# S5 state operators multiplied in turned layout from a table of power factors, instead of turned tile by tile

## What is computed

```python
lam_bar = jnp.exp(lam * dt)
b_bar = ((lam_bar - 1.0) / lam)[..., None] * b
...
bu = jnp.einsum("gnp,btgp->btgn", b_bar, u_chunk.astype(jnp.complex64))
_, xs = lax.associative_scan(binop, (a, bu), axis=1)
xs = xs + pow_t[None] * state[:, None]
y = jnp.real(jnp.einsum("gpn,btgn->btgp", c, xs))
```

## Time and profile before

| | us |
|---|---|
| median of 3 runs (2041.51 to 2043.51) | 2042.86 |
| the profiled execution's own time | 2042.9 |
| its span in the trace | 2041.2 |
| PE busy | 2001.8 (98% of the span) |
| DVE busy | 1583.4 (78%) |
| ACT busy | 1127.8 (55%) |
| POOL busy | 575.6 (28%) |
| tile 0 of down projection 0 starts on PE at | 899.1 |
| its last product ends at | about 1153.7 |

### The profile page before, as it was taken

How to read it: one execution, slowest core, us unless ns; L and a number is a source line. 1 busy time by engine, 2 the same in 40 slices (tenths; PEclk the granted TensorE clock), 3 DMA queues, 4 the chain that set the end, 5 groups by cost and what they waited for, 6 DMA issues and landing times.

```text
span 2041.2 us, 40986 instructions
## 1 busy us (share of the span) xinstructions
PE 2001.8 (98%) x13240; PEld 1747.0 (86%) x13240; DVE 1583.4 (78%) x2216; ACT 1127.8 (55%) x1655; POOL 575.6 (28%) x725
## 2 busy tenths in 40 slices
PE   7999999999999999999999889999999999999998
PEld 7877888888888888888888788888888888888886
DVE  7976678987888888878888887788888888865554
ACT  6544455466666656655555435665665655644443
POOL 8999014930000000037666682100000000001110
PEclk9999999999999999999999999999999999999999
DMA  6554535566666555557777995555555555566664
GB/s 239 164 186 166 165 125 172 189 194 206 213 213 200 188 191 186 188 167 238 234 235 236 309 244 189 189 200 189 186 189 190 186 191 189 182 185 192 186 192 133
DMA packets 147453, 398.82 MB, mean 195 GB/s; under 512 B 23344, under 2 KB 48688, under 8 KB 147392
## 3 DMA queue, kind: packets, MB, share of 16 engines
q1 hardware_dynamic: 126752, 379.30, 57.9%
q10 hardware_dynamic: 20640, 18.75, 2.8%
HBM read 377.02 MB, written 18.87 MB: 194 GB/s over the span
## 4 chain that ended last, share of the span: by engine, by line
PE 86%; POOL 8%; DVE 3%; issue 1%; ACT 1%; DMA 1%; ACTq 0%; SPq 0%; DVEq 0%; POOLq 0%
PE bank L389 50%; PE bank L388 25%; PE bank L385 3%; PE bank L386 1%; DVE lo L365 1%; PE bank L2092 1%; PE bank L2094 1%; PE bank L2093 1%; POOL nt L733 1%; DMA uu<-yg 1%; POOL ut L958 1%; POOL nt L734 1%; POOL nt L732 1%; POOL nt L735 1%; ACT hi L358 0%
## 5 line engine op out<-in xcount | busy, mean ns | idle before, releaser
L365 DVE TENSOR_TENSOR lo<-raw,hi 128x1024 fp32r<-128x1024 f32 x698 | 890.0, 1281 | 184.1 <-ACT hi L358 171.0
L358 ACT ACTIVATE hi<-raw 128x1024 fp32r<-128x1024 f32 x698 | 733.9, 1057 | 389.8 <-PE bank L389 332.9
L389 PE MATMUL bank<-aa,hi 128*128 128x512 f32 x2544 | 890.1, 392 | 0.0
L389 PE MATMUL bank<-xx,hi 128*128 128x512 f32 x2236 | 783.9, 392 | 0.0
L388 PE MATMUL bank<-aa,lo 128*128 128x256 f32 x2544 | 711.7, 280 | 0.0
L388 PE MATMUL bank<-xx,lo 128*128 128x256 f32 x2236 | 626.5, 280 | 0.9 <-DVE lo L365 0.9
L389 PEld LDWEIGHTS bank<-aa,hi 128*128 128x128 f32 x2544 | 477.4, 188 | 100.5
L389 PEld LDWEIGHTS bank<-xx,hi 128*128 128x128 f32 x2236 | 419.6, 188 | 87.3
L388 PEld LDWEIGHTS bank<-aa,lo 128*128 128x128 f32 x2544 | 478.7, 188 | 6.2 <-DVE lo L365 0.3
L388 PEld LDWEIGHTS bank<-xx,lo 128*128 128x128 f32 x2236 | 421.1, 188 | 8.4 <-DVE lo L365 2.2
L403 ACT ACTIVATE lowt<-bank 128x256 f32<-128x256 f32 x212 | 81.1, 383 | 208.6 <-PE bank L389 202.0
(11 more groups left out here) (384 smaller groups left out, 1902.6 us busy)
## 6 DMA issues: line engine op xcount, KB each, us to landing
raw<-in_up SPq DMA_DIRECT2D x344, 512.0 KB, 3.2
raw<-in_down SPq DMA_DIRECT2D x160, 448.0 KB, 3.5
raw<-in_w_in SPq DMA_DIRECT2D x98, 512.0 KB, 4.2
raw<-in_w_out SPq DMA_DIRECT2D x32, 512.0 KB, 3.3
raw<-in_down SPq DMA_DIRECT2D x32, 512.0 KB, 4.3
raw<-in_glu SPq DMA_DIRECT2D x32, 512.0 KB, 3.8
s_c<-cp ACTq DMA_DIRECT2D x16, 256.0 KB, 3.4
s_p<-ut ACTq DMA_DIRECT2D x32, 128.0 KB, 5.6
```

What stands on the lines that cost most here:

```text
L358: A.activation(hi[:, s, :], raw[:, s, :], ACT.Copy).then_inc(hi_done, 1)
L365: V.tensor_tensor(lo[:, s, :], raw[:, s, :], hi[:, s, :].bitcast(f32), SUB).then_inc(lo_done, 1)
L389: last = TE.matmul(bank[:, :], hi[:, s, w], x2(k)[:, :, :], start=False, stop=k == total - 1)
```

## The change

- A table of factors `coef * power` for all states is made once on POOL (24 small instructions, in the up projection of layer 0, behind the rotation tables), turned once on PE (four transposes inside tile 0, `factors_turn`), copied by ACT and stored to a DRAM tensor `s5_f` (`turn_factors`).
- For each tile, SP loads the turned factors (two DMAs of 64 partitions, broadcast) and the input `b` in turned layout (a new input array `s5_bt`, one DMA, broadcast) into `ut` (`load_pf`): 2 KB to each partition from either, 512 KB in all. The loads of tile kt stand in SP's queue right behind `load_bc` of tile kt+2, and wait until POOL has made the state operator of tile kt-2. For the last pair of tiles they stand elsewhere: those of tile 14 behind those of tile 13, ahead of the fetches of tile 15, and those of tile 15 between the fourth and the fifth fetch of tile 15 (`inside`).
- POOL multiplies the state operator straight in turned layout (`state_powers`: one 128x512 product, one 128x256 difference, two 128x256 products, one 128x256 sum), two tiles behind `input_powers`.
- The four transposes of every `kt_turn` go, and so does ACT's 128x512 copy. ACT stores `pt` with one DMA (`store_p`), ahead of the copies of the convolution kernel (`store_k`).

```diff
+            def load_pf(i, s):
+                kt = 2 * i + s
+                for x in range(2):
+                    sp.wait_ge(s5_dma_p[x], X_LOADED + 16)
+                sp.wait_ge(s5_pt_new, kt + 1)
+                n = 2 * 4 * S5_N
+                for w in range(2):
+                    sp.dma_start(ut4[S5_N * w:S5_N * (w + 1), s, :],
+                                 s5_f[w, bass.ds(kt * T5, T5), :].unsqueeze(0).broadcast_to([S5_P, T5, n])
+                                 ).then_inc(pf_full[s], 16)
+                sp.dma_start(ut4[:, 2 + s, :], t["s5_bt"][:, bass.ds(kt * n, n)].unsqueeze(1).broadcast_to(
+                    [2 * S5_P, T5, n])).then_inc(pf_full[s], 16)
...
-            fetch_down("down0", B_DN0, before=load_bc, start=1)
+            fetch_down("down0", B_DN0, before=load_bc, start=1, inside=lambda: load_pf(KT // 2 - 1, 1))
...
                             if before is not None and first and j == RING - 1:
                                 before(i, m)
+                            if inside is not None and isinstance(i, int) and 2 * i + m == KT - 1 and j == RING - 1:
+                                inside()
...
+                if not (isinstance(i, int) and i == 0):
+                    load_pf(i - 1, s)
+                    if isinstance(i, int) and kt == KT - 1:
+                        load_pf(i, 0)
...
-                for part in range(2):
-                    for d in range(2):
-                        ins = G.tensor_tensor(
-                            pq_pt[:, d], bbar[:, s, :, d, :].unsqueeze(3).broadcast_to([P, 4, S5_P, T5]),
-                            pow_in[:, pairs, :, (part + d) % 2].unsqueeze(2).broadcast_to([P, 4, S5_P, T5]), MUL)
...
+            def state_powers(kt):
+                s = kt % 2
+                g.wait_ge(pf_full[s], X_LOADED + 48 * (kt // 2) + 48)
+                if kt >= 2:
+                    g.wait_ge(s5_dma_p[s], X_LOADED + 16 * (kt // 2) + 16)
+                chain(G.tensor_tensor(sumt[:, :, :], f_in[:, s], b_in[:, s], MUL))
+                chain(G.tensor_tensor(pt[:, s, 0, :], sumt[:, 0, :], sumt[:, 1, :], SUB))
+                for d in range(2):
+                    ins = G.tensor_tensor(sumt[:, d, :], f_in[:, s, d], b_in[:, s, 1 - d], MUL)
+                chain(ins)
+                G.tensor_tensor(pt[:, s, 1, :], sumt[:, 0, :], sumt[:, 1, :], ADD).then_inc(s5_pt_new, 1)
...
             for kt in range(KT):
                 input_powers(kt)
+                if kt >= 2:
+                    state_powers(kt - 2)
+                if kt == KT - 1:
+                    state_powers(kt - 1)
                 if kt >= 1:
                     tile_squares(kt - 1)
                     add_skip(kt - 1)
+            state_powers(KT - 1)
...
-                a.wait_ge(s5_p_out, kt + 1)
-                half = 4 * S5_N
-                for part in range(2):
-                    a.dma_start(s5_p[kt, :, half * part:half * (part + 1)].rearrange("(w x) n -> x w n", w=2),
...
+                if not first:
+                    store_p(i - 1, m)
+                if glu_next:
+                    store_p(i, 0)
                 if not (first and m == 0):
-                    store_p_t(*last_kt)
+                    store_k(*last_kt)
...
-                for m in range(4):
-                    last = TE.transpose(pb[0][:, m * P:(m + 1) * P], pt[:, s, m, :, :].rearrange("p a n -> p (a n)"),
-                                        ident[:, :])
```

More of the change, by code:

```diff
@@ L40 @@
 OP_SLOTS, ROT_SLOTS = 4, 8
+X_LOADED = 16
 OUT_PARTS = [(0, 1), (1, 4), (4, 8), (8, 12), (12, 16)]
@@ L315, in hybrid_encoder @@
         bc_full = [sem("bc_full0"), sem("bc_full1")]
-        s5_dma_p, s5_dma_t = sem("s5_dma_p"), [sem(f"s5_dma_t{s}") for s in range(2)]
+        fac_turned = sem("fac_turned")
+        pf_full, s5_dma_p, s5_dma_t = x_in[0:2], x_in[2:4], [sem(f"s5_dma_t{s}") for s in range(2)]
         s5_dma_c = [sem("s5_dma_c0"), sem("s5_dma_c1")]
@@ L511, in fetch_columns, with fetch_down @@
                     fetch(b0, 4, 0, j, w[base + j, :, :], BW)
-            def fetch_down(name, b0, before=None, start=0):
+            def fetch_down(name, b0, before=None, start=0, inside=None):
                 w = t[name]
@@ L526, in pair @@
                                 before(i, m)
+                            if inside is not None and isinstance(i, int) and 2 * i + m == KT - 1 and j == RING - 1:
+                                inside()
                 for i in range(start):
                     pair(i)
-                with sp.Fori(start, KT // 2) as i:
+                end = KT // 2 if inside is None else KT // 2 - 1
+                with sp.Fori(start, end) as i:
+                    pair(i)
+                for i in range(end, KT // 2):
                     pair(i)
@@ L878, in _ @@
             G.tensor_scalar(rot_s[:, :, 0], rho[:, 0, 1, :], -1.0, None, MUL).then_inc(rot_new, 1)
+            pw = powers.rearrange("p (k m) j z -> p k m j z", m=4)
+            fr, fi = (coef[:, d, :].rearrange("p (k m) -> p k m", m=4) for d in range(2))
+            for r in range(T5):
+                pr, pi = (pw[:, :, :, T5 - r, d] for d in range(2))
+                for x, (a, b) in enumerate(((fr, pr), (fi, pi), (fr, pi), (fi, pr))):
+                    ins = G.tensor_tensor(fac_tmp[:, x, r], a, b, MUL)
+            chain(ins)
+            for r in range(T5):
+                G.tensor_tensor(fac_v[:, :, r, 0, :], fac_tmp[:, 0, r], fac_tmp[:, 1, r], SUB)
+                ins = G.tensor_tensor(fac_v[:, :, r, 1, :], fac_tmp[:, 2, r], fac_tmp[:, 3, r], ADD)
+            ins.then_inc(s5_pt_new, 2)
             g.wait_ge(block_used, B_DN0)
             G.memset(k_win[:, :, :], 0.0).then_inc(x_free, 1)
-            for j in range(T5):
-                ins = G.tensor_scalar(pow_in[:, :, j, :], powers[:, :, T5 - j, 0:2], 1.0, None, MUL)
-            chain(ins)
             g.wait_ge(al_new, FT)
@@ L1273, in diagonal, with turn_factors, store_p, store_k @@
                 ins.then_inc(s5_bd_new, 1)
-            def store_p_t(i, s):
+            def turn_factors():
+                a.wait_ge(fac_turned, 1)
+                A.activation(fac_t, pb[4][:, :], ACT.Copy).then_inc(fac_turned, 1)
+                a.wait_ge(fac_turned, 2)
+                for w in range(2):
+                    a.dma_start(s5_f[w, :, :].rearrange("(q k) (x n) -> (k x) q n", q=4, n=S5_N),
+                                fac_t.rearrange("p (q w n) -> p q w n", q=4, w=2)[:, :, w, :]
+                                ).then_inc(s5_dma_p[w], 16)
+            def store_p(i, s):
+                kt = 2 * i + s
+                a.wait_ge(s5_pt_new, kt + 3)
+                a.wait_ge(s5_dma_p[s], X_LOADED + 16 * i + 16)
+                a.dma_start(s5_p[kt, :, :], pt[:, s, :, :].rearrange("p d n -> p (d n)")).then_inc(s5_dma_p[s], 16)
+            def store_k(i, s):
                 kt = 2 * i + s
                 a.wait_ge(s5_kt_turned, kt + 1)
-                if not (isinstance(i, int) and kt == 0):
-                    a.wait_ge(s5_dma_p, 32 * kt)
                 if not (isinstance(i, int) and i == 0):
                     a.wait_ge(s5_dma_t[s], 16 * i)
-                A.activation(pt_t.rearrange("p (w m n) -> p m w n", w=2, m=4),
-                             pb[0][:, :].rearrange("p (m w n) -> p m w n", m=4, w=2), ACT.Copy)
                 k = pb[2][:, 0:S5_P * T5].rearrange("p (c r) -> p c r", r=T5)
@@ L1306, in down_and_store @@
                 last_kt = (i, 0) if m else (i - 1, 1)
-                if not (first and m == 0):
+                if first and m == 0:
+                    turn_factors()
+                else:
                     gained(*last_kt)
@@ L2281, in ffn, with factors_turn @@
                     return
-                down(0, 0)
+                def factors_turn(k):
+                    if k == DOWN_BLOCKS[0]:
+                        p.wait_ge(s5_pt_new, 2)
+                        for q in range(4):
+                            last = TE.transpose(pb[4][:, q * P:(q + 1) * P], fac[:, q * P:(q + 1) * P], ident[:, :])
+                        last.then_inc(fac_turned, 1)
+                down(0, 0, step=factors_turn)
                 def first_turn(k):
@@ L2308, in kt_turn @@
                     for part in range(2):
-                        TE.matmul(pb[2][32 * m:32 * m + 32, 0:T5 * S5_P], bd[:, s, m, part, :],
-                                  cp[:, s, part, m, :], start=part == 0, stop=part == 1, skip_group_check=True)
-                for m in range(4):
-                    last = TE.transpose(pb[0][:, m * P:(m + 1) * P], pt[:, s, m, :, :].rearrange("p a n -> p (a n)"),
-                                        ident[:, :])
+                        last = TE.matmul(pb[2][32 * m:32 * m + 32, 0:T5 * S5_P], bd[:, s, m, part, :],
+                                         cp[:, s, part, m, :], start=part == 0, stop=part == 1,
+                                         skip_group_check=True)
```

40 lines of the change are left out of this document (20 added, 20 removed).

## The result

The changed kernel takes 2053.49 us (median of 6, 2052.86 to 2054.5), the kernel before on the same chip 2042.18 (6 runs). The ratio is 1.0053, with a 95% interval of 1.0043 to 1.0063: **11 us slower**, outside the range that was forecast. The profiled execution has a span of 2051.5 us against 2041.2, so the trace has 10.3 of these 11 us.

The account below looks back on a forecast made before the run. PE was taken to bound the down projection of layer 0, with POOL's delay counting in the S5 stage behind it. Sum: 2042.9 - 5.7 (transposes) + 6.8 (late residual) + 1.3 (POOL) = 2045.3 us, range 2037.0 to 2051.0.

Parts of the forecast that it names:

- What goes from PE: Down projection of layer 0: dropping four transposes saves 0.41 us a turn, net 14 turns, 5.7 us (4.5 to 8.3).
- no PE idle time in tiles 1 to 13: Sign to check in the projection: PE never idle there, with the distance between tiles falling from 15.88 to 15.47 us.
- First wait: Tile 14's loads hold block 90 in SP's queue until pass 12 ends; PE's turn 1.6 us late (0 to 2.4).
- Second wait: Tile 15's loads hold block 94 until pass 13 ends; tile 15's residual 6.8 us late (4.1 to 10.2).
- POOL ahead of the S5 stage: Tile 15's pass stands before POOL's first S5 product and delays the stage by 1.3 us (0.7 to 3).
- The rival on the clock: PE's clock falls to half in the gap of tile 15, adding 2.9 us: 2048.2 us; chance 0.07.
- The rule on the shared port: DVE and POOL block each other; with DVE starved the second pass would take 4.1 us, the sum 0.5 smaller.
- the short end: Lower bound for one POOL pass making a tile's state operator: 4.1 us, against 6.2 at the top.
- The rival that every tile pays: DMA at 0.90 makes PE's turn wait some 0.5 us in each of 14 tiles: about 2051 us; chance 0.08.
- The rival of long passes: POOL's operations stay at 1.60 us, landings take 4.5; second wait 10.2, POOL 3: about 2050.5 us; chance 0.2.
- The range: Whole kernel's forecast time between 2037.0 and 2051.0 us, taking in the covered-fetch case and the long passes.
- the sum's own high end: Whole kernel with all high ends: 2042.9 - 4.5 + 10.2 + 3 = 2051.6 us.

Follow-up runs that it names:

- run 8: run 7 with PE's loop over tiles 2 to 13 written out instead of rolled; 2037.9 us, ratio 0.9977.
- Experiments 3: The changed kernel with only the loads for tile 14 moved, behind block 93 together with those for tile 15; 2047.4 us, ratio 1.0025.
- 10: The changed kernel with SP's order kept and POOL's and ACT's order of run 7; 2044.9 us, ratio 1.0009.
- run 9: run 8 with ACT's store of tile 14's operators moved behind the root for the norm; 2038.9 us, ratio 0.9979.
- run 4: The changed kernel with unread products on PE: 21 ahead of the turn of tile 14, 16 ahead of the wait for block 94; 2054.4 us, ratio 1.0056.
- run 7: The changed kernel with both tiles' loads issued later, POOL's pass 13 ahead of the skip, squares before pass 14, ACT's two stores moved; 2039.2 us, ratio 0.9984.
- runs 5: The kernel before with the four transposes of every turn left out, operators stale, no new loads; 2037.5 us, ratio 0.9977.
- runs 2: The changed kernel with only the loads for tile 15 moved, behind block 97; 2049.8 us, ratio 1.0037.

## Why the prediction was wrong

The mechanism was right: block 90 late, pass 13 late, block 94 late, and PE idle in two places, each where it was put. So was the direction, a kernel slower by 2.4 us (2045.3 against 2042.9). The size was not, and the steps that failed are the terms of the sum. The forecast counts the chain in the times of the kernel before and takes the saving off at the end; in these terms the two tiles lost 14.3 us instead of 6.8.

- **"What goes from PE": 5.7 us.** The turns saved 4.04. The distance fell to 15.47 us only where the loop does not jump; at its five back edges it is 15.8, with 0.25 us of "issue" (run 8: the jump), so 5 x 0.33 = 1.7 us did not come. One pair of rows had been read and taken for all. By tile 14 PE was 4.95 ahead, 0.8 short of the forecast and not 1.7, because of the 0.91 us from ahead of the first turn: luck. The sign "no PE idle time in tiles 1 to 13" failed by these 0.25 us.
- **"First wait": 1.6 us. This is the step that failed most.** 5.19 were measured. The bounds (0 to 2.4) were too tight since nearly all its terms went up together: POOL from the end of ACT's copy to the pass 4.0 us instead of 2.35 (`input_powers` had one difference of 1.38, where 0.32 was the length before); the pass 6.8 instead of 6.2; the loads' issues 2.4 us from the pass's end to block 90 instead of 1.3 (a load's issue took 0.6, a fetch's 0.33 had been the model); from block 90's issue to ACT's split 4.6 instead of 3.6. Only ACT's part came out shorter, 3.65 instead of 4.1. Together these are 3.9 us; the turn had 0.3 to spare.
- **"Second wait": residual 6.8 us late.** It was 14.3 in the forecast's terms. It inherits the 3.9 us of the first wait and adds some 3.6 of its own: copy to pass 4.4 instead of 2.35 (POOL's small products and the skip took 2.03 and 1.34 us, beside DVE's splits of the late blocks, where they had taken 1.04 and 0.46), the loads' issues 1.96 and the landing 4.25 instead of 1.3 and 3.6, and 0.4 behind block 94. With the 0.8 of the saving, and less the 0.3 of the next term, this is 8.0 us, by which the profiled execution missed the sum (2053.3 against 2045.3). The pass itself was 4.45, forecast 4.6. As a chain this was right; what its bounds left out is that an error in the first hold returns in full in the second. Experiments 3 and 10 show the coupling.
- **"POOL ahead of the S5 stage": 1.3.** 0.96, for another reason: POOL was not what came last there, DVE's square was longer (1.38 instead of 0.42) with POOL's pass beside it. That the pass made it longer is read from the two lengths, not tried. The right size is in part luck: POOL was free only 0.26 us before that product, so with a short square POOL would have bound, for some 0.7. It does bind once the holds are gone (run 9).
- **The rival on the clock** (0.07, 2.9 us): both gaps (5.19 and 4.01 us) were followed by the half clock (0.50 in 1138 to 1142 and in 1157 to 1160), the first one too, which the rival had not named, but here it cost at most 1.2 us (run 4). Leaving it out of the sum was nearly right by size, not by the argument. The Trainium skill, page "TensorE: Matmul & The Clock Gate", section "Why this matters for your kernels", warns that a long gap between bursts of products brings the half clock back. The trace agrees with it for these gaps; in the kernel before, idle time of 3.37 us in 1168 to 1174 was followed by 1.00. That the clock falls does not say that time is lost: what PE waits for next decides.
- **The rule on the shared port.** The Trainium skill, page "SBUF — State Buffer", section "SBUF: two separate sides", says that DVE and GpSimd lock each other out. The trace agrees: pass 13, with DVE starved, had its 128x256 difference and sum at 0.74 us each; pass 12, with DVE's splits beside it, had one at 1.73. Pass 13 as a whole took 4.45 all the same, not the 4.1 of the short end, since its products were longer than in the rows they were taken from (1.28 and 1.45 instead of 1.06 and 1.26).
- **The rival that every tile pays** came nearest by its number (about 2051) and was wrong in its reason: PE had no idle time for data from 931 to 1117, with the DMA engines at 0.86 to 0.88.
- **The rival of long passes** (2050.5) was half right. Its landings of 4.5 held (4.6 and 4.25 to ACT's split), its long passes only for the first (6.8 us, but 4.45 for the second); it too had no term for POOL's work ahead of the passes, which grew by 1.65 and 2.1 us.
- **The range** ended at 2051.0, under the sum's own high end of 2051.6 (the low end takes 0.8 us for POOL where its range begins at 0.7, on which nothing hangs). The measured time lies above both ends.

## What to carry to other kernels

A load that must wait, put into an in-order queue in front of a weight fetch, costs not its own time but that of everything that its release waits for; follow that chain over all queues, and look whether it comes back through the fetch that it delays (here fetch, ACT's split, ACT's copy, POOL's pass, next load). When the terms of such a chain come from rows of the kernel before, widen them together: the change that creates the chain also makes its neighbours slower. And a saving on the bound engine has to be brought through the end of its stage: here some 4 to 5 us needed three more moves (SP, POOL, ACT), after which 3.3 arrived by the ratio of run 7 (4.7 with PE's loop written out, run 8).

## What had not been expected of the hardware

- PE's loop has a price of its own: 0.25 us of idle time at each back edge and 0.33 us in the distance of the tiles (runs 5 and 8). It did not show while the four transposes stood ahead of the jump (every distance 15.88 or 15.89 in the kernel before). The Trainium skill, page "Advanced Engine Details and Errata", section "Control Flow Timing", gives about 0.11 us for a compare and branch. The measured loss is two to three times that.
- Issuing a load that repeats its source over 64 partitions took SP 0.54 to 0.71 us. One fetch of a weight block took 0.33 in the loop and 0.43 to 0.59 in the last pair of tiles, where SP's program is written out in the changed kernel.
- Idle gaps of PE of 6.46 and 5.36 us were followed by a granted clock of 0.50 in runs 2 and 10 too. Filling the first gap with products kept it at 1.00; a gap of 2.89 us that stayed open was followed by 0.51 (run 4).
- Open: in the S5 stage PE has idle times of "issue" of 0.3 to 3.4 us at changing places in every version, the kernel before included. Which part of the scatter between versions (2037.5 for run 5, 2037.9 and 2038.9 for runs 8 and 9) they make was not tried.
